# A second block's output projection computed from high and low parts, with single row buffers

## The reference

```python
mixed = jnp.concatenate([o_a, o_b], axis=-1).astype(x.dtype)
x = x + jnp.einsum("bse,ed->bsd", mixed, w_out[l])
h2 = rms_norm(x, ffn_norm[l])
x = x + hierarchical_moe(h2, w_router_group[l], w_router_expert[l], w_gate[l], w_up[l], w_down[l])
```

## Time and profile before

| what | value |
|---|---|
| median of 3 runs | 2123.31 us (2123.18 to 2125.99) |
| span of the profiled execution | 2126.7 us (its own device time isn't given) |
| TensorE busy | 1956.5 us, 92% |
| VectorE, ScalarE, GpSimd busy | 38%, 29%, 29% |
| recurrence, first step after the input projection to the first expert product | about 1188 to 1582 us |
| expert stage | about 1582 to 2087 us |
| DMA, whole span | 371.8 MB, 175 GB/s; 417 to 425 GB/s in most of the expert stage |

### The profile page before, as it was taken

One profiled execution on the slowest core, in us unless ns is written; L12 is line 12 of the kernel. 1 busy time (PEld: TensorE's weight loads), 2 busy tenths in 40 slices (PEclk: granted clock), 3 DMA queues, 4 the chain that ended last, 5 costly groups with the idle time before them and its releaser, 6 DMA issues. The chain is left out here.

```text
span 2126.7 us, 31150 instructions
## 1 busy us (share of the span) xinstructions
PE 1956.5 (92%) x12049; PEld 1379.7 (65%) x12049; DVE 808.6 (38%) x1461; ACT 615.9 (29%) x1324; POOL 606.6 (29%) x619
## 2 busy tenths in 40 slices
PE   8999999999999989999999899999979888888885
PEld 7998887787787767878887666666563222322222
DVE  5223256666453443440112456676531211111114
ACT  5333145555323432331112432232212111111111
POOL 1226387332211110010114676665211111111102
PEclk9999999999999999999999999999989989999998
DMA  5103461211420253622332422211659999999996
GB/s 208 52 31 140 147 200 26 51 26 46 150 83 28 45 122 67 83 60 94 94 119 86 161 83 95 81 56 55 260 224 417 425 424 425 423 422 420 418 383 263
DMA packets 101730, 371.80 MB, mean 175 GB/s; under 512 B 17429, under 2 KB 40154, under 8 KB 74714
## 3 DMA queue, kind: packets, MB, share of 16 engines
q1 hardware_dynamic: 82592, 323.55, 42.6%
q0 software_dynamic: 16704, 42.10, 5.1%
q10 hardware_dynamic: 2298, 4.23, 0.5%
HBM read 321.47 MB, written 65.14 MB: 182 GB/s over the span
## 5 line engine op out<-in xcount | busy, mean ns | idle before, releaser
L2907 PE MATMUL ps<-w_gu,rows_t 128*64 128x512 f32 x1024 | 260.4, 667 | 58.1 <-DMA w_gu<-w_up 56.5
L2907 PEld LDWEIGHTS ps<-w_gu,rows_t 128*64 128x64 f32 x1024 | 79.2, 152 | 216.1 <-issue 155.8
L3165 POOL DMA_INDIRECT y_d<-y_out,asg_i x32 | 32.2, 1006 | 429.9 <-DVE y_out L2991 414.7
L2982 DVE TENSOR_TENSOR act_s<-act_g,ps 128x256 f32<-128x256 f32 x32 | 13.5, 421 | 326.1 <-ACT act_g L2973 326.1
L2334 PE MATMUL ps<-w_o,mix_t 128*128 128x512 f32 x256 | 124.3, 616 | 0.0
L2925 PE MATMUL ps<-w_d,act_tt 128*64 128x512 f32 x512 | 116.9, 598 | 0.5 <-issue 0.5
L1120 ACT ACTIVATE prob<-ps,stats 128x1024 f32<-128x1024 f32 (+7 forms) x128 | 94.5, 738 | 62.1 <-DVE stats L1083 61.7
L2973 ACT ACTIVATE act_g<-ps 128x256 f32<-128x256 f32 x32 | 12.3, 384 | 323.7 <-PE ps L2907 323.7
L310 PE MATMUL ps<-tk_lo,h_hi 128*128 128x512 f32 x256 | 100.4, 392 | 3.0 <-DVE tk_lo L302 3.0
L310 PE MATMUL ps<-tk_hi,h_lo 128*128 128x512 f32 x256 | 100.3, 392 | 0.0
L310 PE MATMUL ps<-tk_hi,h_hi 128*128 128x512 f32 x256 | 100.2, 392 | 0.0
(11 more groups left out here) (477 smaller groups left out, 4389.6 us busy)
## 6 DMA issues: line engine op xcount, KB each, us to landing
w_gu<-w_gate SPq DMA_DIRECT2D x64, 1024.0 KB, 20.0
w_gu<-w_up SPq DMA_DIRECT2D x64, 1024.0 KB, 23.5
w_d<-w_down SPq DMA_DIRECT2D x64, 1024.0 KB, 23.6
w_tk<-w_in SPq DMA_DIRECT2D x5, 2048.0 KB, 13.6
proj_d<-tok_o POOLq DMA_DIRECT2D x40, 256.0 KB, 2.3
tk_in<-proj_d SPq DMA_DIRECT2D x8, 1280.0 KB, 5.9
w_ch<-w_in SPq DMA_DIRECT2D x12, 512.0 KB, 10.2
proj_d<-conv_o POOLq DMA_DIRECT2D x12, 512.0 KB, 3.9
```

What stands on the lines that cost most here:

```text
L2907: mm = pe.matmul(ps[half, 2, :].rearrange("p (g n) -> p g n", g=2), rows_t[:, k, half], w_gu[q][:, h, :, k, :], start=(k == 0), stop=(k == ...
L2982: v.tensor_tensor(act_s[:, :].rearrange("q (k p) -> q k p", k=2), by_k(act_g[:, :]), by_k(ps[:, 2, DE:]), ALU.mult).then_inc(s_acts, 1)
L3165: pool.indirect_dma_start(out=y_d, out_offset=bass.IndirectOffsetOnAxis(ap=idx, axis=0), in_=y_out[q][:, :], in_offset=None, bounds_check= ...
```

## The change

Four things are changed together.

- The projection multiplies float32r parts: high part of `mixed` by low part of the weights, high by high, and low by high. ScalarE writes `mix_hi` from PSUM, VectorE subtracts it from the same bank into `mix_lo` and frees the bank (`mix_low`, in its piece `e_p0`). TensorE's `e_p0` holds the 16 products with `mix_hi` for the first half, `e_p1` the 8 with `mix_lo`, the other pieces three products for each k. The orders and the banks stay as they are.
- The weights are loaded raw in three pieces, after all stores of the last product. ScalarE writes their scaled high part, VectorE the low part in step 1 (`low_weights`, pieces `n_ut3` to `n_ut6`).
- `qkv_in`, `tk_in` and `qk_r` have one buffer each. The loads are split (queries and keys, values and gates) and stand at other places of SP's queue; the rotation waits for the former block's turn.
- The tiles move, 12 KB lower in SBUF, and the scratch for GpSimd's DMA descriptors is set to 4096 bytes (the default is 16384). The first experts' loads are regrouped.

```diff
         def sem(name):
             return ctx.enter_context(nc.semaphore(name))
 
-        base_off = 16512
+        base_off = 4224
 
         def sb(name, shape, off, dt=F32):
...
+        s_b, s_bd, k_dk, p_t = (take(x, H4) for x in ("s_b", "s_bd", "k_dk", "p_t"))
+
+        w_hi = sb("w_o2_hi", [P, KD, D], at(64), F32R)
+        W_LO = ((0, 4, at(96)), (4, 2, at(112)), (6, 2, at(152)))
+        w_raw = [sb(f"w_o2_raw{k}", [P, n, D], o) for k, n, o in W_LO]
+        w_low = [sb(f"w_o2_lo{k}", [P, n, D], o, F32R) for k, n, o in W_LO]
+
+        def w_part(parts, k):
+            i = 0 if k < 4 else 1 if k < 6 else 2
+            return parts[i][:, k - W_LO[i][0], :]
+
+        take = area(at(160), 229344 - base_off)
+        mixed = take("mixed", H8)
...
+            for q in range(4):
+                wait(sp, s_tst[q], 16 * 10)
+            for (k, n, _), part in zip(W_LO, w_raw):
+                sp.dma_start(part[:, :, :], A["w_out_2"][0].rearrange("(k p) n -> p k n", p=P)[:, k:k + n, :]).then_inc(s_wo2, 16)
 
         def load_qkv(sp, t):
-            sp.dma_start(qkv_in[t % 2][:, :], proj_d[t * P:(t + 1) * P, 0:3 * NA]).then_inc(s_ldA[t % 2], 16)
-
-        def load_tk(sp, t):
+            dve_a.wait(sp, "qkn", t - 1)
+            pool_n.wait(sp, "vb", t - 1)
+            sp.dma_start(qkv_in[:, :], proj_d[t * P:(t + 1) * P, 0:3 * NA]).then_inc(s_ldA, 16)
+
+        def token_rows(t, c, n):
+            at_ = CONV_CH + c * BANK
+            return proj_d[t * P:(t + 1) * P, at_:at_ + n * BANK]
+
+        def load_qk(sp, t):
+            pool_n.wait(sp, "sinx", t - 1)
             wait(sp, s_tst[t % 4], 16 * (9 + t // 4))
-            sp.dma_start(tk_in[t % 2][:, :, :].rearrange("p a n -> p (a n)"), proj_d[t * P:(t + 1) * P, 3 * NA:]).then_inc(s_ldB[t % 2], 16)
+            sp.dma_start(tk_in[:, 1:3, :].rearrange("p a n -> p (a n)"), token_rows(t, 1, 2)).then_inc(s_ldQ, 16)
+
+        def load_vg(sp, t):
+            if t > 0:
+                full(sp, "SR", t - 1)
+                pool_o.wait(sp, "og", t - 1)
+            wait(sp, s_tst[t % 4], 16 * (9 + t // 4))
+            sp.dma_start(tk_in[:, 0, :], token_rows(t, 0, 1)).then_inc(s_ldV, 16)
+            sp.dma_start(tk_in[:, 3:5, :].rearrange("p a n -> p (a n)"), token_rows(t, 3, 2)).then_inc(s_ldV, 16)
 
         def loaded(eng, sems, t):
             eng.wait_ge(sems[t % 2], 16 * (t // 2) + 16)
+
+        def rows_loaded(eng, semaphore, t):
+            eng.wait_ge(semaphore, (32 if semaphore is s_ldV else 16) * (t + 1))
 
         def d_sp(sp):
             for s in range(T + 3):
@@ -2098,25 +2124,22 @@
                         loaded(sp, s_x4st, t - 2)
                         dve_l.wait(sp, "hn", t - 2)
                     sp.dma_start(res2[t % 2][:, :], x1_d[t * P:(t + 1) * P, :]).then_inc(s_res2[t % 2], 16)
-                t = s + 2
-                if t < T:
-                    dve_a.wait(sp, "qkn", t - 2)
-                    pool_n.wait(sp, "vb", t - 2)
-                    load_qkv(sp, t)
                 t = s + 1
                 if 2 <= t < T:
-                    full(sp, "SR", t - 2)
-                    pool_o.wait(sp, "og", t - 2)
-                    load_tk(sp, t)
+                    load_qkv(sp, t)
+                    load_qk(sp, t)
+                if 1 <= s < T:
+                    load_vg(sp, s)
                 if s == T:
                     copied(sp, f"U{LEV - 1}", T - 1)
+                    pool_n.wait(sp, "rot", T - 1)
                     full(sp, "ST", T - 2)
-                    dve_o.wait(sp, "mixed", T - 2)
-                    load_pair(sp, 0)
+                    load_gu(sp, 0)
                 if s == T + 1:
                     dve_o.wait(sp, "mixed", T - 1)
                     copied(sp, "SR", T - 1)
-                    full(sp, "ST", T - 1)
+                    copied(sp, "ST", T - 1)
+                    load_d(sp, 0)
                     load_pair(sp, 1)
...
@@ -2322,18 +2345,34 @@
                 turn4("M0", t, mixed[:, 0:4, :])
                 turn4("M1", t, mixed[:, 4:8, :])
 
-            def project(t, j, ks):
-                job = f"OUT{j}"
-                if ks[0] == 0:
-                    copied(pe, "M0", t)
-                    copied(pe, "M1", t)
-                    pe.wait_ge(s_wos, KD)
-                    begin(pe, job, t)
-                b = ps[:, place[job, t][0], :]
-                for k in ks:
-                    mm = pe.matmul(b, mix_t[:, k, :], w_o2[:, k, j * BANK:(j + 1) * BANK], start=(k == 0), stop=(k == KD - 1))
-                if ks[-1] == KD - 1:
-                    filled(mm, job, t)
+            def first_half_high(t):
+                act_e.wait(pe, "h0", t)
+                act_e.wait(pe, "h1", t)
+                pe.wait_ge(s_wos, KD)
+                pe.wait_ge(s_wol, WOL0 + KD)
+                b = begin(pe, "OUT0", t)
+                for k in range(KD):
+                    pe.matmul(b, mix_hi[:, k, :], w_part(w_low, k)[:, 0:BANK], start=(k == 0), stop=False)
+                    pe.matmul(b, mix_hi[:, k, :], w_hi[:, k, 0:BANK], start=False, stop=False)
+
+            def first_half_low(t):
+                copied(pe, "M0", t)
+                copied(pe, "M1", t)
+                b = ps[:, place["OUT0", t][0], :]
+                for k in range(KD):
+                    mm = pe.matmul(b, mix_lo[:, k, :], w_hi[:, k, 0:BANK], start=False, stop=(k == KD - 1))
+                filled(mm, "OUT0", t)
+
+            def second_half(ks):
+                def piece(t):
+                    b = begin(pe, "OUT1", t) if ks[0] == 0 else ps[:, place["OUT1", t][0], :]
+                    for k in ks:
+                        pe.matmul(b, mix_hi[:, k, :], w_part(w_low, k)[:, BANK:], start=(k == 0), stop=False)
+                        pe.matmul(b, mix_lo[:, k, :], w_hi[:, k, BANK:], start=False, stop=False)
+                        mm = pe.matmul(b, mix_hi[:, k, :], w_hi[:, k, BANK:], start=False, stop=(k == KD - 1))
+                    if ks[-1] == KD - 1:
+                        filled(mm, "OUT1", t)
+                return piece
 
             def l_turn(j):
...
             def a_sums(t):
-                loaded(act, s_ldA, t)
+                rows_loaded(act, s_ldA, t)
                 pool_a.wait(act, "ms", t - 1)
                 pool_n.wait(act, "rot", t - 1)
-                act_a.done(head_squares(sin_x, lambda h: qkv_in[t % 2][:, h * HD:(h + 1) * HD], ss_qk), "sq")
+                act_a.done(head_squares(sin_x, lambda h: qkv_in[:, h * HD:(h + 1) * HD], ss_qk), "sq")
 
...
             def e_turn(t):
-                copy("M0", t, mix_t[:, 0:4, :])
-                copy("M1", t, mix_t[:, 4:8, :])
+                for j in range(2):
+                    b = read(act, f"M{j}", t)
+                    act_e.done(act.activation(flat4(mix_hi[:, 4 * j:4 * j + 4, :]), b, ACT.Copy), f"h{j}")
 
...
-                        act.wait_ge(s_wo2, 16)
+                        act.wait_ge(s_wo2, 48)
                         act.wait_ge(s_gab, 32)
                     for k in (2 * i, 2 * i + 1):
                         g = 0 if k < AH else 1 + k - AH
-                        act.activation(w_o2[:, k, :], w_o2[:, k, :], ACT.Copy, scale=gain_ab[:, g:g + 1]).then_inc(s_wos, 1)
+                        act.activation(w_hi[:, k, :], w_part(w_raw, k), ACT.Copy, scale=gain_ab[:, g:g + 1]).then_inc(s_wos, 1)
                 return piece
 
...
 
+            def mix_low(t):
+                for j in range(2):
+                    act_e.wait(v, f"h{j}", t)
+                    b = read(v, f"M{j}", t)
+                    part = slice(4 * j, 4 * j + 4)
+                    freed(low(v, flat4(mix_lo[:, part, :]), b, flat4(mix_hi[:, part, :])), f"M{j}", t)
+
+            def low_weights(i, then):
+
+                def piece(t):
+                    then(t)
+                    if t != 1:
+                        return
+                    for k in (2 * i, 2 * i + 1):
+                        v.wait_ge(s_wos, k + 1)
+                        g = 0 if k < AH else 1 + k - AH
+                        v.scalar_tensor_tensor(w_part(w_low, k), w_part(w_raw, k), gain_ab[:, g:g + 1], w_hi[:, k, :].bitcast(F32),
+                                               ALU.mult, ALU.subtract).then_inc(s_wol, 1)
+                return piece
+
             def add_half(j):
                 def piece(t):
...
             pieces = dict(a_norm=a_norm, n_decay=n_decay, n_scores=n_scores, n_first=n_first, o_read=o_read, o_out=o_out, o_scores=o_scores,
-                          o_mix=o_mix, o_state=o_state, o_end=o_end, e_x0=add_half(0), e_x1=add_half(1), l_hn=l_hn, l_logits=l_logits, d_logits=l_logits, q_max=r_max, q_group=r_group, q_top1=r_top1, q_top2=r_top2,
+                          o_mix=o_mix, o_state=o_state, o_end=o_end, e_p0=mix_low, e_x0=add_half(0), e_x1=add_half(1), l_hn=l_hn, l_logits=l_logits, d_logits=l_logits, q_max=r_max, q_group=r_group, q_top1=r_top1, q_top2=r_top2,
```

(18 more changed lines are left out.)

69 lines of the change are left out of this document (33 added, 36 removed).

## The result

The changed kernel takes **2143.86 us** (median of 4 runs, 2138.97 to 2144.81), the kernel before 2124.16 in the same comparison. The ratio is 1.0086, 95% interval 1.0072 to 1.0101: 19.7 us slower. Forecast were 2137.9 us and 2125 to 2146. The profiled execution took 2144.66 us, its span is 2143.0.

What follows compares the result with a forecast made beforehand. The expert stage was taken as bound by its weight stream, the recurrence ahead by TensorE. Steps 1 and 2 (0), five steps (+13.0) and last steps (+1.6) gave +14.6 on 2123.3: 2137.9 us, range 2125 to 2146.

Steps and rivals of the forecast that it cites:

- The products: Projection on TensorE: three part products take 0.681 us for 0.864, saving 2.9 us a row block.
- The hand-over: Bank 6 of PSUM: TensorE's e_p0 waits for VectorE's subtraction behind hn, a stall of 3.3 us.
- The clock: TensorE's granted clock falls in each 3.3 us stall, adding 1.5 us a step.
- Rival 1: Stall at bank 6 comes but TensorE's clock stays: +5.6 us, 2129 us; chance 0.18.
- Rival 3: TensorE's clock stays low longer at each stall: 6 x 1.6 us more, 2148 us; chance 0.10.
- Rival 2: Bank 6 comes free in time, so the products' savings win, 2.2 us a step: 2107 us; chance 0.10.
- Through the step: Recurrence steps 3 to 7: 1.1 us longer from stall less savings, 2.6 with the clock, 13.0 over five steps.
- Steps 1 and 2: First two recurrence steps: low parts, later weight load and product savings sum to about 0 (-2 to +2 us).
- so 1.5 us: Step 1: TensorE's turn waits 1.5 us for qk_n, delayed by VectorE's low parts of the weights.
- The last steps: Step 8's stall and clock delay the router, the last block's products save 2.9 us: together +1.6 us.
- One for one: Expert stage: whatever delays or advances the waiting expert load at 1589.15 us reaches the end in full.
- so 0: Smaller descriptor scratch of GpSimd's DMAs: costs nothing, as a chunk's 13 us of work lies between convolution stores.

Runs made afterwards that it cites:

- experiment 1: Changed kernel with the piece that makes hn moved behind the first pair of subtractions on every engine's order: 2122.39 us, ratio 0.9989 to the kernel before.
- experiment 8: Changed kernel with the mixture turned ahead of the scores, first subtraction ahead of VectorE's scores, hn behind the first products: 2109.15 us, ratio 0.9934.
- experiment 4: Changed kernel with three unused products filling TensorE's stall ahead of e_p0 in blocks 0 to 5: 2136.0 us, ratio 1.0055.
- experiment 7: Changed kernel without VectorE's eight low-part instructions of step 1; products take the high part again, giving another result: 2136.83 us, ratio 1.0058.
- storage alone: Changed kernel's storage, loads and grouping with fp32 products, no low parts, both banks freed by ScalarE: 2118.59 us, ratio 0.9976.
- experiment 10: Kernel of experiment 8 with 6 MB of expert weights loaded ahead of the store of block 6's hn, the rest after it landed: 2105.18 us, ratio 0.9908.
- experiment 9: Kernel before the change with only the descriptor scratch of GpSimd's DMAs cut to 4096 bytes: 2120.63 us, ratio 0.9979.
- experiment 12: Kernel of experiment 8 with the tail's loads of experiment 10 and the weights' low parts made in halves, the second halves spread over step 2: 2103.44 us, ratio 0.9905.
- experiment 5: Kernel before the change with one added wait: GpSimd's first rotated product waits for TensorE's turn of the former block's keys: 2120.42 us, ratio 0.9982.
- experiment 6: Changed kernel with only the third expert pair's loads held until block 6's hn has landed: 2143.77 us, ratio 1.0082.

## Why the prediction was right, and where not

The direction, the range and the main mechanism held: the hand-over of bank 6 behind `hn`, and the clock. The point was 6.0 us low, and that the time fell into the range was also luck. Steps 1 and 2 and the last steps lost 4.2 and 7.2 us more than forecast; the five steps lost 2.3 less, and the smaller scratch, put at nothing, gave 4.5 back. Without that alone the time would have been some 2148, outside the range.

- **The products.** 0.681 us for three was right: `e_p1` takes 2.0 us, the last block's run 12.95 for a forecast of 12.6.
- **The hand-over.** 3.3 us of stall behind `hn`; the trace has 16.2 us in the five steps, 3.24 each. Experiments 1 and 8 take it away and the time with it. Right.
- **The clock.** 1.5 us a step forecast, 1.73 by experiment 4. Rival 1 (the clock stays) is out. Rival 3 wanted 1.6 us more at each stall. The five steps' mean of 0.96 makes some 19 us at the lower level (1.2 GHz), 3.9 a step, and the price above is what it cost: out too, for the five steps (step 8 is below). Rival 2's bank that comes free in time is experiment 8: 2109.15 us for its 2107, where the steps' 2.2 us were right; that the total agrees is luck, since the scratch, GpSimd's wait, step 1 and the tail were not in it.
- **Through the step.** +2.6 forecast, +2.14 measured against the kernel before. This is two terms: +2.96 against the kernel with the same storage (48.36 - 45.40), and -0.8 for GpSimd's wait. What failed here is "The wait of the rotated rows for `TK` ends before GpSimd gets there": it ends 0.34 us after, and it helped.
- **Steps 1 and 2.** About 0 forecast, +4.2 measured. The term "so 1.5 us" for the low parts is 6.2 by experiment 7, which keeps the load: it treated VectorE's queue alone. The 1 us for the later weight load was nothing: storage alone, with that load, takes 76.66 from `B` to the first store, and the kernel before with GpSimd's wait, without it, the same. The cheaper products gave 1.2 (76.66 to 75.47) where the forecast had 2.4, and GpSimd's wait, which the forecast had put at nothing, gave another 0.8.
- **The last steps.** +1.6 forecast from step 7's store to the waiting load, +8.8 measured: 3.9 in step 8, -0.7 in step 9, 5.6 in the tail. "The loads of the second expert pair's stage are regrouped, but all precede 1589.15" looked at when the loads are needed and not at what is behind them in the DMA queues. The tail's 5.6 is TensorE's wait for `hn`, 9.5 us for 3.9. The storage-alone kernel has 8.6 there and +4.1 us in its tail, and experiment 10 takes 5.1 away. The other 1.4 is not the stall's alone: experiment 8 has none, still waits 9.6, and its tail keeps 0.7 of it. A likely reason, not tested by itself, is the shorter run of the last block, which brings the store of `hn` sooner behind the same loads (18.0 us, 18.7 with storage alone). The 3.2 of steps 8 and 9 are twice what the forecast had, and are the hand-over: step 8 is 26.31 us in experiment 1 and 24.53 in experiment 8, where nothing stalls. Its stall was as forecast, its clock cost more:

```profile
1524.12 0.76 PE L2355 MATMUL ps<-w_o_lo,mix_hi 128*128 128x512 f32 x1 [3.51 <-DVE mix_lo L302]
...
1530.17 0.39 PE L2356 MATMUL ps<-w_o_hi,mix_hi 128*128 128x512 f32 x1
```

The sixteen products of step 8's `e_p0` take some 6.3 us where 3.65 is full speed, so 2.6 for the forecast's 1.5.
- **The rest.** "One for one" from 1589.15 to the end, and "so 0" for the scratch. The load came 23.65 us later and the time 19.7: the smaller scratch gives back 4.5 at the very end (experiment 9).

The marks and the scratch account for the measured times. For the change 422.58 - 398.83 - 4.5 = 19.3 against 19.7; for experiments 4, 7 and 8 11.4, 12.7 and -16.1 against 11.3, 12.2 and -15.4; for experiment 12 -21.8 against -20.2. In no run do the two differ by more than 1.8 us. The profiled execution of before was some 3 us longer behind the last mark than most others (537.55 - 4.5 against 530), and its span stands 3.4 us above the median that the prediction started from.

## What to carry to other kernels

Where a bank or buffer passes from one engine's release to another's, look at what stands ahead of the new releaser in its own queue: here one `hn` of 2 us cost 3.3 us of waiting and 1.7 us of clock in each step, more than the cheaper products gained. With both subtractions ahead of it the loss of 20 us was gone, and with the mixture turned earlier too it was a gain of 15. When work is added to an engine, price it with the engines that share its ports, and when loads are regrouped, count the bytes ahead of the next small store that somebody waits for. And test the parts of a change by themselves: its storage half alone was faster than the kernel before.

## What was not expected of the hardware

- VectorE with two SBUF inputs and GpSimd held each other up in both directions (experiments 5 and 7): 0.23 to 1.25 us, 1.23 to 3.36 on VectorE, 0.24 to 1.14 and 1.67 to 4.11 on GpSimd. A wait of 0.34 us on GpSimd took 0.8 us off each step.
- A store of 512 KB took 2.6 us where the DMA engines had just gone idle, and 7.3 to 8.9 where 8 MB of loads, issued on the other queue from 16 to 19 us earlier on, were still under way, whether new ones followed (8.2 with the change) or not (8.4 in experiment 6).
- The size of GpSimd's descriptor scratch shows at the end of the program: 7.2 us from the last store's issue to the end with the default size, 2.6 to 2.7 with 4096 bytes.
